# Attention: the local part's steps spread over three more places on three engines, column sums, scores and transposes one step later on TensorE

## The chip, the cores and the metric

The kernel runs on one core of a Trainium2 chip. The metric is the device time of one execution, in microseconds (us). The kernel before took 2866.6 us (median of 3 runs, 2866.42 to 2877.24).

The engines are TensorE (PE in the profile; PEld is its weight load), VectorE (DVE), ScalarE (ACT), GpSimd (POOL) and SyncE (SP), which only issues the weight DMAs here. Each works through its own list of instructions in program order and waits on semaphores that the others raise.

## The reference, cut to what matters

The program is two transformer-like blocks of two layers each, on 512 tokens of width 1024. The change touches the attention of the second block alone. Each of its two layers has 8 heads of stick-breaking attention and 8 heads of local ("sliding window") attention with a sink:

```python
def stick_breaking_attention(q, k, v):      # 8 heads of 64
    z = q @ k.T * scale                      # per block of 128 queries
    log_keep = where(strict, -softplus(z), 0)
    tail = cumsum(log_keep, reverse=True) - log_keep
    w = where(strict, exp(log_sigmoid(z) + tail), 0)
    return w @ v

def sliding_window_sink_attention(q, k, v, sinks):   # window 128
    scores = where(valid, q @ k_band.T * scale, -inf)
    probs = softmax(concat([scores, sink]))[..., :-1]
    return probs @ v_band

for l in range(DEPTH):
    h = rms_norm_2(x, mix_norm_g[l])
    sb_q, sb_k, sb_v, sw_q, sw_k, sw_v, gate_logits = split(h @ w_in[l])
    y_sb = stick_breaking_attention(sb_q, sb_k, sb_v) @ w_branch_sb[l]
    q = apply_rope(rms_norm_2(sw_q, q_norm_g[l])); k = apply_rope(rms_norm_2(sw_k, k_norm_g[l]))
    y_swa = sliding_window_sink_attention(q, k, sw_v, sinks[l]) @ w_branch_swa[l]
    x = x + (gate0 * y_sb + gate1 * y_swa) @ w_out[l]
    x = x + square(relu(rms_norm_2(x, mlp_norm_g[l]) @ w_up[l])) @ w_down[l]
```

## The kernel before, in words

All activations stay on chip, transposed: 128 channels on the partitions, 512 tokens along the row. Weights come in units of 128x1024 elements. SyncE loads a unit, ScalarE rounds it to its high part (`w_hi`, line 882), VectorE subtracts to get the low part (`w_lo`, line 1350), and TensorE makes each product in three matmuls: high by high, low by high, high by low (lines 399 to 401). A unit is 24 such matmuls.

An attention layer works through four pairs, numbered 0 to 3, each with two heads of the stick-breaking part (`stick`) and two of the local part (`window`, its heads called half 0 and half 1). Beside them run the projections that later work needs, the fill: five units in each pair, cut into 20 parts of 6 matmuls. When a unit is done, ScalarE makes a `w_hi` and VectorE stores the result (line 1826) and makes a `w_lo`.

The three are Python generators, and every `yield` ends a step. `interleave` gives step i of n the place `first + (last - first) * (i + 1) / n` on a line from 0 to 1, sorts all steps by place, and writes the instructions out in that order. It is called on TensorE, ScalarE and VectorE separately, with the same numbers. `STICK_STEPS` is 21 over 0 to 1, `WINDOW_STEPS` is 17 over 0 to 0.8, and the fill has 20 over 0.1 to 1. So the order on each engine is fixed by how many steps come before an instruction in its generator.

The steps of `window`, with their lines on the page:

- ScalarE squares the local queries (L1250) once VectorE has stored the pair's fourth unit; TensorE sums over the columns (L775); ScalarE makes the inverse root (L890, L892).
- VectorE scales the queries (L1779) and rotates them in six operations (L1767 to L1773); TensorE makes the scores (L789 to L794).
- VectorE takes the maximum (L1790, L1793); ScalarE the exponentials (L1263, L1265); VectorE the probabilities (L1798 to L1803); TensorE transposes them (L805); ScalarE copies them (L1271); TensorE makes the output (L811, L812); ScalarE copies it (L1275). Then half 1 does the same from the scores on.

The steps of `stick` are the transposes of v (L726), and for each of 8 tiles, n = 0 to 7, of 128, 256, 384 and 512 columns twice over: logits (L736, L737) after the copies of q and k (L1738, L1739), three ScalarE operations (L1229 to L1233, in the text e(n)), the softplus on VectorE (L1747), sums (L1755), the log weights (L745, L748), their exponential (L1238), and the output (L756).

Of the kernel before, what the change touches and what calls it, by code (L numbers as in the profile page):

```python
# [136 lines left out]
class Done:  # L137
# [5 lines left out]
    def mark(self, *event):  # L143
        self.n += 1
        self.plan[event] = self.n
        return self.sem, 1
# [4 lines left out]
    def now(self):  # L151
        return self.sem, self.n
# [28 lines left out]
class Kernel:  # L181
# [47 lines left out]
    def vcol(self, name, i=0, n=1):  # L229
        at = VEC[name] + i  # L230
        return self.vec[:, at:at + n]
# [112 lines left out]


STICK_STEPS = 1 + 2 * (2 * TC + 1) + 1 + 1
WINDOW_STEPS = 2 + 2 + 2 * 6 + 1
STICK_ORDER = [(half, j) for half in range(2) for j in reversed(range(TC))]
Z_BANK_OF = {2: 0, 4: 2, 5: 1, 6: 4, 7: 3}

# [1 line left out]
def filling(fill, parts):  # L352
    for _ in range(parts - 1):
        fill.part()
        yield
    fill.part()


def pair_tasks(stick, window, fill):
    return ((stick, STICK_STEPS, 0, 1), (window, WINDOW_STEPS, 0, 0.8),  # L360
            (filling(fill, len(fill.units) * PARTS), len(fill.units) * PARTS, 0.1, 1))


# [14 lines left out]
def score_view(k, n):  # L378
    return k.bank[6 + n // 2][:, (n % 2) * 2 * P:(n % 2) * 2 * P + 2 * P]
# [10 lines left out]
def pe_program(k):  # L390
# [380 lines left out]

    def window(layer, m):
        at = (layer, m)
        pe.wait_ge(*act_done.at("wq_sq", *at))
        pe.matmul(bank[6][:], k.halves, k.sq, start=True, stop=True).then_inc(*mark("wq_sum", *at))  # L775
        yield
        yield
        yield
        yield
        for half in range(2):  # L780
            r = slice(half * 64, half * 64 + 64)
            if half == 0:
                pe.wait_ge(*dve_done.at("wq", *at))
            else:
                pe.wait_ge(*act_done.at("wo", *at, 0))
            for n in range(TC):
                s = score_view(k, n)
                if n == 0:
                    pe.matmul(s[:, 0:P], k.id_b[:], k.mask_b[:, P:2 * P], start=True, stop=True)  # L789
                    pe.matmul(s[:, P:2 * P], k.id_b[:], k.mask_b[:, 3 * P:4 * P], start=True, stop=False)  # L790
                    mm = pe.matmul(s[:, P:2 * P], k.wq[r, 0:P], k.wk[r, 0:P], start=False, stop=True)
                else:
                    pe.matmul(s, k.id_b[:], k.mask_b[:, 2 * P:4 * P], start=True, stop=False)
                    mm = pe.matmul(s, k.wq[r, n * P:n * P + P], k.wk[r, (n - 1) * P:(n + 1) * P],  # L794
                                   start=False, stop=True)
            mm.then_inc(*mark("scores", *at, half))
            yield
            yield
            yield
            yield  # L800
            pe.wait_ge(*dve_done.at("probs", *at, half))
            for n in range(TC):
                for s in range(2):
                    to = ((n % 2) * 2 + s) * P
                    mm = pe.transpose(bank[6 + n // 2][:, to:to + P], k.p_t[:, n, s * P:s * P + P], k.ident)  # L805
            mm.then_inc(*mark("pT", *at, half))
            yield
            pe.wait_ge(*act_done.at("pT", *at, half))
            for n in range(TC):
                if n > 0:  # L810
                    pe.matmul(bank[6][r, n * P:n * P + P], k.wvt[:, n - 1, r], k.pT[:, n, 0:P], start=True, stop=False)  # L811
                mm = pe.matmul(bank[6][r, n * P:n * P + P], k.wvt[:, n, r], k.pT[:, n, P:2 * P], start=n == 0,  # L812
                               stop=True)
            mm.then_inc(*mark("wo", *at, half))
            yield
# [53 lines left out]
def act_program(k):  # L869
# [18 lines left out]
    def inverse_root(dst, src, scale, *event):  # L888

        act.activation(dst, src, ACT.Ln, scale=scale, bias=k.eps_col[:]).then_inc(*mark())  # L890
        act.wait_ge(*now())
        act.activation(dst, dst, ACT.Exp, scale=-0.5).then_inc(*mark(*event))  # L892
# [354 lines left out]
    def window(layer, m):  # L1247
        at = (layer, m)
        act.wait_ge(*dve_done.at("fill", UNIT["pair", layer, m, 3]))
        act.activation(k.sq, k.lands[3][:], ACT.Square).then_inc(*mark("wq_sq", *at))  # L1250
        yield
        act.wait_ge(*pe_done.at("wq_sum", *at))
        inverse_root(k.rstd[:], bank[6][:], 1.0 / 64, "wq_root", *at)
        yield
        yield
        yield
        for half in range(2):
            r = slice(half * 64, half * 64 + 64)
            yield
            yield  # L1260
            act.wait_ge(*dve_done.at("max", *at, half))
            for n in range(TC):
                act.activation(k.p_t[:, n, :], score_view(k, n), ACT.Exp, bias=k.st[:, 1, n:n + 1],  # L1263
                               accum_out=k.st[:, 2, n:n + 1]).then_inc(*mark())
            act.activation(k.st[:, 3, :], k.st[:, 1, :], ACT.Exp,  # L1265
                           bias=vcol("sinks2", layer * 8 + m + half * 4)).then_inc(*mark("exps", *at, half))
            yield
            yield
            act.wait_ge(*pe_done.at("pT", *at, half))
            for b in range(2):  # L1270
                act.activation(k.pT[:, 2 * b:2 * b + 2, :], bank[6 + b][:].rearrange("p (n s) -> p n s", n=2),  # L1271
                               ACT.Copy).then_inc(*mark("pT", *at, half))
            yield
            act.wait_ge(*pe_done.at("wo", *at, half))
            act.activation(k.wo[r, :], bank[6][r, :], ACT.Copy).then_inc(*mark("wo", *at, half))  # L1275
            yield
        act.wait_ge(*now())
        act.activation(k.y_hi[:, m + 4, :], k.wo[:], ACT.Copy).then_inc(*mark("att_y", layer, m + 4))
# [60 lines left out]
def dve_program(k):  # L1339
# [128 lines left out]
    def rope(x, rot, hd):  # L1468
        dve.wait_ge(*now())
        dve.tensor_tensor(rot[0:64, :], x[64:128, :], k.sin128[64:128, :], ALU.mult).then_inc(*mark())  # L1470
        dve.wait_ge(*now())
        dve.tensor_tensor(rot[64:128, :], x[0:64, :], k.sin128[0:64, :], ALU.mult).then_inc(*mark())
        dve.wait_ge(*now())
        dve.tensor_tensor(x[:], x[:], k.cos128[:], ALU.mult).then_inc(*mark())
        dve.wait_ge(*now())
        dve.tensor_tensor(x[:], x[:], rot[:], ALU.add).then_inc(*mark("rope", hd))
# [298 lines left out]
    def window(layer, m):  # L1775
        at = (layer, m)
        yield
        dve.wait_ge(*act_done.at("wq_root", *at))
        dve.scalar_tensor_tensor(k.wq[:], k.lands[3][:], vcol("q_gain2", layer), k.rstd[:], ALU.mult,  # L1779
                                 ALU.mult).then_inc(*mark())  # L1780
        yield
        rope(k.wq, k.rot).then_inc(*mark("wq", *at))
        yield
        yield
        for half in range(2):
            yield
            sink = vcol("sinks2", layer * 8 + m + half * 4)
            dve.wait_ge(*pe_done.at("scores", *at, half))
            for b in range(2):
                dve.tensor_reduce(k.st[:, 0, 2 * b:2 * b + 2], bank[6 + b][:].rearrange("p (n s) -> p n s", n=2),  # L1790
                                  AX.X, ALU.max).then_inc(*mark())
            dve.wait_ge(*now())
            dve.tensor_scalar(k.st[:, 1, :], k.st[:, 0, :], sink, -1.0, ALU.max,  # L1793
                              ALU.mult).then_inc(*mark("max", *at, half))
            yield
            yield
            dve.wait_ge(*act_done.at("exps", *at, half))
            dve.tensor_tensor(k.st[:, 4, :], k.st[:, 2, :], k.st[:, 3, :], ALU.add).then_inc(*mark())  # L1798
            dve.wait_ge(*now())
            dve.reciprocal(k.st[:, 4, :], k.st[:, 4, :]).then_inc(*mark())  # L1800
            dve.wait_ge(*now())
            for n in range(TC):
                dve.tensor_scalar(k.p_t[:, n, :], k.p_t[:, n, :], k.st[:, 4, n:n + 1], None,  # L1803
                                  ALU.mult).then_inc(*mark("probs", *at, half))
            yield
            yield
            yield
        dve.wait_ge(*act_done.at("att_y", layer, m + 4))
        dve.tensor_tensor(k.y_lo[:, m + 4, :], k.wo[:], k.y_hi[:, m + 4, :].bitcast(F32),
                          ALU.subtract).then_inc(*mark("att_y", layer, m + 4))  # L1810
# [293 lines left out]
```

## Time and profile before

| | before |
|---|---|
| median of 3 runs | 2866.6 us |
| lowest, highest | 2866.42, 2877.24 us |
| the profiled execution | 2872.39 us |
| its span in the trace | 2870.8 us |
| TensorE busy | 2780.5 us (97%), 12462 matmuls |
| VectorE busy | 1509.9 us (53%) |
| ScalarE busy | 1166.3 us (41%) |
| GpSimd busy | 113.0 us (4%) |

The span is the time between the first and the last instruction of the trace; the execution's time has another 1.6 us around it. Busy times are sums of instruction durations. "Granted clock" is TensorE's clock as a share of full speed, 2.4 GHz, in a stretch; its other level is half of that, 1.2 GHz. A timeline row gives the start, the duration, and in brackets how long the engine was idle before it and who released it.

### The profile page before, as it was taken

What the parts mean: (1) busy time and instruction counts of PE and PEld (TensorE: products, weight loads), DVE (VectorE), ACT (ScalarE), POOL (GpSimd) and SP (SyncE); (2) the same over time, 40 slices, a digit from 0 to 9 for tenths busy, and PEclk for the clock granted to TensorE, in tenths of its full rate; (3) what the DMA queues carried; (4) which work ended last, traced back from release to release, by engine and by line L of the source; (5) the groups of instructions that cost most, each with busy time, mean ns of one, the idle gap of its engine ahead of it and who ended that gap; (6) DMA issues with size and microseconds to landing.
All of it is one profiled execution on the core that took longest, in us unless ns stands there. A gap on an engine that the chain in (4) does not pass through costs nothing.

```text
span 2870.8 us, 30831 instructions
## 1 busy us (share of the span) xinstructions
PE 2780.5 (97%) x12462; PEld 2196.8 (77%) x12462; DVE 1509.9 (53%) x2077; ACT 1166.3 (41%) x1736; POOL 113.0 (4%) x79
## 2 busy tenths in 40 slices
PE   8999999999999999999999999999999999999999
PEld 6888778888877888886555788888865557888887
DVE  4566667565676746575343454343544334543433
ACT  6444344333474424354444433332444444333322
POOL 2333110000010000000000000000000000000000
PEclk9999999999999999999999999999999999999999
DMA  4111112332322322331111222232311112222322
GB/s 165 52 63 52 52 59 96 103 96 96 103 95 94 103 95 96 103 103 59 37 44 37 81 96 95 96 103 96 96 59 37 45 37 81 96 96 96 102 97 74
DMA packets 66812, 235.65 MB, mean 82 GB/s; under 512 B 7408, under 2 KB 8176, under 8 KB 66672
## 3 DMA queue, kind: packets, MB, share of 16 engines
q1 hardware_dynamic: 62064, 226.00, 24.2%
q10 hardware_dynamic: 4608, 7.70, 0.8%
q8 instruction: 99, 1.62, 0.2%
q14 instruction: 41, 0.34, 0.0%
HBM read 231.57 MB, written 2.10 MB: 81 GB/s over the span
## 4 chain that ended last, share of the span: by engine, by line
PE 87%; DVE 5%; ACT 4%; issue 2%; POOL 1%; ACTq 0%; DVEq 0%
PE bank L399 25%; PE bank L401 25%; PE bank L400 25%; PE bank L745 1%; ACT w_hi_k L882 1%; PE bank L794 1%; PE bank L756 1%; DVE w_lo_k L1350 1%; PE bank L736 1%; PE bank L748 1%; PE bank L805 1%; PE bank L549 1%; PE bank L812 1%; POOL q_mix L1907 1%; POOL v_mix L1907 1%
## 5 line engine op out<-in xcount | busy, mean ns | idle before, releaser
L399 PE MATMUL bank<-x_hi_k,w_hi_k 128*128 128x512 f32 x2152 | 874.2, 406 | 16.4 <-DVE x_lo_k L1357 16.0
L401 PE MATMUL bank<-x_hi_k,w_lo_k 128*128 128x512 f32 x2152 | 844.3, 392 | 0.0
L400 PE MATMUL bank<-x_lo_k,w_hi_k 128*128 128x512 f32 x2152 | 842.4, 391 | 0.0
L882 ACT ACTIVATE w_hi_k<-raw_k 128x1024 fp32r<-128x1024 f32 x431 | 454.2, 1058 | 946.3 <-PE bank L401 946.3
L1350 DVE TENSOR_TENSOR w_lo_k<-raw_k,w_hi_k 128x1024 fp32r<-128x1024 f32 x431 | 531.4, 1233 | 183.7 <-ACT w_hi_k L882 183.6
L399 PEld LDWEIGHTS bank<-x_hi_k,w_hi_k 128*128 128x128 f32 x2152 | 407.7, 189 | 105.2 <-DVE x_lo_k L1357 18.6
L401 PEld LDWEIGHTS bank<-x_hi_k,w_lo_k 128*128 128x128 f32 x2152 | 406.4, 189 | 87.2
L400 PEld LDWEIGHTS bank<-x_lo_k,w_hi_k 128*128 128x128 f32 x2152 | 407.5, 189 | 84.6 <-issue 4.1
L399 PE MATMUL bank<-y_hi_k,w_hi_k 128*128 128x512 f32 x1136 | 446.4, 393 | 10.8 <-DVE w_lo_k L1350 7.7
L400 PE MATMUL bank<-y_lo_k,w_hi_k 128*128 128x512 f32 x1136 | 443.2, 390 | 0.0
L401 PE MATMUL bank<-y_hi_k,w_lo_k 128*128 128x512 f32 x1136 | 443.2, 390 | 0.0
L1378 DVE TENSOR_TENSOR h_k<-h_k,bank 128x512 f32<-128x512 f32 x136 | 93.3, 686 | 324.2 <-PE bank L401 323.8
L399 PEld LDWEIGHTS bank<-y_hi_k,w_hi_k 128*128 128x128 f32 x1136 | 214.0, 188 | 57.4 <-DVE w_lo_k L1350 9.0
L401 PEld LDWEIGHTS bank<-y_hi_k,w_lo_k 128*128 128x128 f32 x1136 | 213.9, 188 | 44.9
L400 PEld LDWEIGHTS bank<-y_lo_k,w_hi_k 128*128 128x128 f32 x1136 | 214.1, 188 | 43.9 <-issue 0.2
L1876 DVE SCALAR_TENSOR_TENSOR rel_att<-bank,scale_k 128x512 f32<-128x512 f32 x64 | 44.3, 692 | 158.9 <-PE bank L401 158.9
L1747 DVE SCALAR_TENSOR_TENSOR sp_t_att<-bank,e_t_att 128x128 f32<-128x128 f32 (+1 forms) x64 | 31.3, 489 | 90.5 <-ACT e_t_att L1233 89.8
L1238 ACT ACTIVATE w_t_att<-bank 128x128 f32<-128x128 f32 (+1 forms) x64 | 28.2, 440 | 118.7 <-PE bank L745 62.5
L1606 DVE SCALAR_TENSOR_TENSOR cv_ffn<-fpad_ffn,vec_k,cv_ffn 128x512 f32<-128x512 f32 x88 | 65.9, 749 | 1.5
L1606 DVE SCALAR_TENSOR_TENSOR cv_att<-fpad_att,vec_k,cv_att 128x512 f32<-128x512 f32 x88 | 65.9, 749 | 1.5
L736 PE MATMUL bank<-q_att,k_att 64*128 64x128 f32 (+3 forms) x128 | 53.5, 499 | 0.0
L1372 DVE TENSOR_TENSOR fpad_att<-bank,scale_k 128x512 f32<-128x512 f32 x44 | 30.3, 688 | 42.3 <-PE bank L401 42.3
(320 smaller groups left out, 2556.6 us busy)
## 6 DMA issues: line engine op xcount, KB each, us to landing
raw_k<-wstream SPq DMA_DIRECT2D x431, 512.0 KB, 3.3
h_k<-xT ACTq DMA_DIRECT2D x8, 256.0 KB, 7.9
outT<-h_k ACTq DMA_DIRECT2D x8, 256.0 KB, 2.8
decay_mix<-constants ACTq DMA_DIRECT2D x4, 256.0 KB, 2.6
levels_mix<-constants ACTq DMA_DIRECT2D x1, 448.0 KB, 9.1
vec_k<-vectors ACTq DMA_DIRECT2D x1, 286.5 KB, 4.5
cos_mix<-constants ACTq DMA_DIRECT2D x1, 256.0 KB, 8.6
sin_mix<-constants ACTq DMA_DIRECT2D x1, 256.0 KB, 8.6
```

Source lines behind the costliest of these rows:

```text
L399: pe.matmul(dst, wh, rh, start=start, stop=False)
L400: pe.matmul(dst, wh, rl, start=False, stop=False)
L401: return pe.matmul(dst, wl, rh, start=False, stop=stop)
L736: pe.matmul(z_view(k, j), k.ak[r, j * P:j * P + P], k.aq[r, j * P:T], start=True, stop=False)
L882: act.activation(k.w_hi[:, u % SPLIT, :], k.raw[:, u % RAW, :], ACT.Copy).then_inc(*hi_done.mark())
L1350: dve.tensor_tensor(k.w_lo[:, u % SPLIT, :], k.raw[:, u % RAW, :], k.w_hi[:, u % SPLIT, :].bitcast(F32), ALU.subtract).then_inc(*k.lo_done ...
L1372: return dve.tensor_tensor(dst, src, k.scale[:], ALU.mult).then_inc(*mark(*event))
L1378: dve.tensor_tensor(k.h[:, m, :], k.h[:, m, :], bank[BANK[name]][:], ALU.add).then_inc(*mark("added", u))
L1606: dve.scalar_tensor_tensor(cv[j][:], pad[j][:, s:s + T], vcol("ffn_conv", w0 + s), cv[j][:], ALU.mult, ALU.add).then_inc(*mark("conv", lay ...
L1747: dve.scalar_tensor_tensor(keys_view(k.sp_t, j), z_view(k, j), 0.0, k.e_t[:, n % 2, 0:T - j * P], ALU.max, ALU.add).then_inc(*mark("softpl ...
L1876: dve.scalar_tensor_tensor(k.rel[:, j, :], bank[i % 4][:], 0.0, k.scale[:], ALU.max, ALU.mult).then_inc(*mark("rel", u))
L1907: pool.tensor_tensor(dst[:], dst[:], k.taps[s], ALU.add).then_inc(*mark("conv", hd, j))
```

## The change

`window` gets three more steps inside and one more at its start, so each of its generators has 21 steps in place of 17, and its last place goes from 0.8 to 0.85. Nothing is added or taken away on any engine; only the order in which the instructions are written out is another. Line numbers below are those of the kernel before; the changed kernel's are 2 to 9 higher in this part.

```diff
@@ -344,7 +344,7 @@
 
 
 STICK_STEPS = 1 + 2 * (2 * TC + 1) + 1 + 1
-WINDOW_STEPS = 2 + 2 + 2 * 6 + 1
+WINDOW_STEPS = 6 + 2 * 7 + 1
 STICK_ORDER = [(half, j) for half in range(2) for j in reversed(range(TC))]
 Z_BANK_OF = {2: 0, 4: 2, 5: 1, 6: 4, 7: 3}
 
@@ -357,7 +357,7 @@
 
 
 def pair_tasks(stick, window, fill):
-    return ((stick, STICK_STEPS, 0, 1), (window, WINDOW_STEPS, 0, 0.8),
+    return ((stick, STICK_STEPS, 0, 1), (window, WINDOW_STEPS, 0, 0.85),
             (filling(fill, len(fill.units) * PARTS), len(fill.units) * PARTS, 0.1, 1))
 
 
@@ -771,8 +771,10 @@
 
     def window(layer, m):
         at = (layer, m)
+        yield
         pe.wait_ge(*act_done.at("wq_sq", *at))
         pe.matmul(bank[6][:], k.halves, k.sq, start=True, stop=True).then_inc(*mark("wq_sum", *at))
+        yield
         yield
         yield
         yield
@@ -794,6 +796,7 @@
                     mm = pe.matmul(s, k.wq[r, n * P:n * P + P], k.wk[r, (n - 1) * P:(n + 1) * P],
                                    start=False, stop=True)
             mm.then_inc(*mark("scores", *at, half))
+            yield
             yield
             yield
             yield
@@ -1254,6 +1257,8 @@
         yield
         yield
         yield
+        yield
+        yield
         for half in range(2):
             r = slice(half * 64, half * 64 + 64)
             yield
@@ -1264,6 +1269,7 @@
                                accum_out=k.st[:, 2, n:n + 1]).then_inc(*mark())
             act.activation(k.st[:, 3, :], k.st[:, 1, :], ACT.Exp,
                            bias=vcol("sinks2", layer * 8 + m + half * 4)).then_inc(*mark("exps", *at, half))
+            yield
             yield
             yield
             act.wait_ge(*pe_done.at("pT", *at, half))
@@ -1775,11 +1781,13 @@
     def window(layer, m):
         at = (layer, m)
         yield
+        yield
         dve.wait_ge(*act_done.at("wq_root", *at))
         dve.scalar_tensor_tensor(k.wq[:], k.lands[3][:], vcol("q_gain2", layer), k.rstd[:], ALU.mult,
                                  ALU.mult).then_inc(*mark())
         yield
         rope(k.wq, k.rot).then_inc(*mark("wq", *at))
+        yield
         yield
         yield
         for half in range(2):
@@ -1802,6 +1810,7 @@
             for n in range(TC):
                 dve.tensor_scalar(k.p_t[:, n, :], k.p_t[:, n, :], k.st[:, 4, n:n + 1], None,
                                   ALU.mult).then_inc(*mark("probs", *at, half))
+            yield
             yield
             yield
             yield
```

First place: TensorE, half 0, around the scores. `wk_att,wq_att` are the scores, `sp_t_att,negs_att` the log weights of tile 0, `q_att,k_att 128x384` the logits of tile 2; `x_hi_k` to `w_lo_k` are the fill. Before:

```order
L401 MATMUL bank<-x_hi_k,w_lo_k 128x512
L789 MATMUL bank<-mask_b_att,id_b_att 128x128
...
L794 MATMUL bank<-wk_att,wq_att 128x256
L745 MATMUL bank<-sp_t_att,negs_att 128x128
L399 MATMUL bank<-x_hi_k,w_hi_k 128x512
...
L401 MATMUL bank<-x_hi_k,w_lo_k 128x512
L736 MATMUL bank<-q_att,k_att 128x384
```

and now:

```order
L401 MATMUL bank<-x_hi_k,w_lo_k 128x512
L745 MATMUL bank<-sp_t_att,negs_att 128x128
L399 MATMUL bank<-x_hi_k,w_hi_k 128x512
...
L401 MATMUL bank<-x_hi_k,w_lo_k 128x512
L791 MATMUL bank<-mask_b_att,id_b_att 128x128
...
L796 MATMUL bank<-wk_att,wq_att 128x256
L736 MATMUL bank<-q_att,k_att 128x384
```

The log weights and one part of the fill stood behind the scores and stand ahead of them now, so the logits follow the scores directly.

Second place: VectorE, half 0, from the maximum to the probabilities. `st_att<-bank` is the maximum, `p_t_att` the probabilities, `sp_t_att<-bank` the softplus of tiles 2 (384) and 3 (512). Before:

```order
L1790 TENSOR_REDUCE st_att<-bank 128x2 x2
L1793 TENSOR_SCALAR st_att<-st_att,vec_k 128x4
L1747 SCALAR_TENSOR_TENSOR sp_t_att<-bank,e_t_att 128x384
L1755 TENSOR_TENSOR sp_t_att<-sp_t_att 128x128
L1798 TENSOR_TENSOR st_att<-st_att 128x4
L1800 RECIPROCAL st_att<-st_att 128x4
L1803 TENSOR_SCALAR p_t_att<-p_t_att,st_att 128x256 x4
L1747 SCALAR_TENSOR_TENSOR sp_t_att<-bank,e_t_att 128x512
```

and now:

```order
L1753 SCALAR_TENSOR_TENSOR sp_t_att<-bank,e_t_att 128x384
L1798 TENSOR_REDUCE st_att<-bank 128x2 x2
L1801 TENSOR_SCALAR st_att<-st_att,vec_k 128x4
L1761 TENSOR_TENSOR sp_t_att<-sp_t_att 128x128
L1753 SCALAR_TENSOR_TENSOR sp_t_att<-bank,e_t_att 128x512
L1806 TENSOR_TENSOR st_att<-st_att 128x4
L1808 RECIPROCAL st_att<-st_att 128x4
L1811 TENSOR_SCALAR p_t_att<-p_t_att,st_att 128x256 x4
```

The maximum went behind the softplus of tile 2, and the probabilities behind that of tile 3.

Third place: ScalarE, half 1, where the exponentials (`p_t_att,st_att`) meet a `w_hi`. Before:

```order
L1263 ACTIVATE p_t_att,st_att<-bank,st_att 128x256 x4
L1265 ACTIVATE st_att<-st_att,vec_k 128x4
L1238 ACTIVATE w_t_att<-bank 128x128
L882 ACTIVATE w_hi_k<-raw_k 128x1024
L1229 ACTIVATE e_t_att<-bank 128x384
```

and now:

```order
L1241 ACTIVATE w_t_att<-bank 128x128
L885 ACTIVATE w_hi_k<-raw_k 128x1024
L1268 ACTIVATE p_t_att,st_att<-bank,st_att 128x256 x4
L1270 ACTIVATE st_att<-st_att,vec_k 128x4
L1232 ACTIVATE e_t_att<-bank 128x384
```

The exponentials of half 1 went behind the `w_hi`, which waits for a unit of the fill.

## Rows read from the trace of the kernel before

**Rows 1.** Waits on TensorE (PE), whole span: total us, times, longest.

```profile
PE bank L789 <- DVE wq_att L1773: 14.6, 8, 1.8
PE bank L805 <- DVE p_t_att L1803: 14.2, 13, 1.5
PE bank L775 <- ACT sq_k L1250: 13.8, 8, 1.7
```

**Rows 2.** Windows: stretch, length, busy us (count) PE, PEld, DVE, ACT, POOL, clock, DMA.

```profile
1318.61:1387.94 69.33, 63.98 (x264) 40.90 (x264) 27.39 (x52) 30.87 (x68) 0.00 (x0) 0.95 0.12 39
1387.94:1459.88 71.94, 66.90 (x265) 42.66 (x265) 27.40 (x52) 30.97 (x68) 0.00 (x0) 0.91 0.11 37
1459.88:1526.45 66.57, 61.01 (x264) 39.29 (x264) 27.39 (x52) 30.76 (x68) 0.00 (x0) 1.00 0.12 40
2110.60:2180.04 69.44, 63.99 (x264) 40.81 (x264) 27.40 (x52) 30.87 (x68) 0.00 (x0) 0.95 0.12 38
2180.04:2246.62 66.58, 61.01 (x264) 39.29 (x265) 27.40 (x52) 30.75 (x68) 0.00 (x0) 1.00 0.12 40
2315.74:2385.00 69.26, 65.42 (x271) 42.31 (x272) 27.03 (x52) 30.44 (x68) 0.00 (x0) 0.95 0.12 39
...
1396.94:1402.24 5.30, 5.30 (x14) 2.36 (x14) 0.27 (x1) 0.00 (x0) 0.00 (x0) 0.53 0.00 0
```

**Rows 3.** Timeline of TensorE, pair 2: start, us, instruction [idle before <- releaser].

```profile
1459.88 1.12 PE L775 MATMUL bank<-sq_k,con_k 128*128 128x512 f32 x2 [1.73 <-ACT sq_k L1250]
...
1461.37 0.48 PE L736 MATMUL bank<-q_att,k_att 64*128 64x128 f32 x2
...
1468.87 0.23 PE L789 MATMUL bank<-mask_b_att,id_b_att 128*128 128x128 bf16 x1 [1.82 <-DVE wq_att L1773]
...
1472.03 0.49 PE L745 MATMUL bank<-sp_t_att,negs_att 128*128 128x128 f32 x2
...
1473.84 0.91 PE L736 MATMUL bank<-q_att,k_att 64*128 64x384 f32 x2
...
1481.58 1.09 PE L805 MATMUL bank<-con_k,p_t_att 128*128 128x128 f32 x8 [0.53 <-DVE p_t_att L1803]
...
1482.50 0.81 PE L745 MATMUL bank<-sp_t_att,negs_att 128*128 128x384 f32 x2
...
1485.07 0.43 PE L812 MATMUL bank<-pT_att,wvt_att 128*64 128x128 f32 x2
...
1501.26 0.91 PE L736 MATMUL bank<-q_att,k_att 64*128 64x384 f32 x2
...
1505.26 1.09 PE L805 MATMUL bank<-con_k,p_t_att 128*128 128x128 f32 x8 [1.49 <-DVE p_t_att L1803]
...
1508.33 0.43 PE L812 MATMUL bank<-pT_att,wvt_att 128*64 128x128 f32 x2
...
1510.00 1.12 PE L736 MATMUL bank<-q_att,k_att 64*128 64x512 f32 x2
```

**Rows 4.** Timeline of ScalarE (ACT), the same pair.

```profile
1476.03 0.53 ACT L1233 ACTIVATE e_t_att<-e_t_att 128x384 f32<-128x384 f32 x1
...
1477.82 0.47 ACT L1263 ACTIVATE p_t_att<-bank,st_att 128x256 f32<-128x256 f32 x1 [1.26 <-DVE st_att L1793]
...
1480.08 0.61 ACT L1229 ACTIVATE e_t_att<-bank 128x512 f32<-128x512 f32 x1
...
1501.43 1.06 ACT L882 ACTIVATE w_hi_k<-raw_k 128x1024 fp32r<-128x1024 f32 x1 [1.18 <-PE bank L401]
```

**Rows 5.** Timeline of VectorE (DVE), the same pair.

```profile
1460.81 0.42 DVE L1739 COPY k_att<-land_k_att 128x512 f32<-128x512 f32 x1
...
1476.24 1.28 DVE L1790 TENSOR_REDUCE st_att<-bank 128x2 f32<-128x512 f32 x2
...
1479.96 0.16 DVE L1798 TENSOR_TENSOR st_att<-st_att 128x4 f32<-128x4 f32 x1 [1.32 <-ACT st_att L1265]
...
1482.05 0.69 DVE L1747 SCALAR_TENSOR_TENSOR sp_t_att<-bank,e_t_att 128x512 f32<-128x512 f32 x1 [0.53 <-ACT e_t_att L1233]
```


## The prediction

> **What bounds the kernel now.** I read the page's busy table first: TensorE is busy nearly all the span, every other engine about half of it or less, so only what TensorE waits for, or how fast it is clocked, can move the time. Then the waits of TensorE. In the attention there are three, and the change moves the instruction behind each: the column sum waits for the squares (13.8 us, 8 times 1.73), the scores for the rotated queries (14.6 us, 8 times 1.82), the transposes for the probabilities (14.2 us, 13 times) [rows 1]. They make 42.6 us, which no reordering can exceed by waits alone.
>
> Then the windows, one for each pair from its column sum to the next one's. They show a second loss. Two pairs ran at a granted clock of 1.00 all through and took 66.57 and 66.58 us, so a pair without disturbance is the same to a hundredth. The others show 0.95 or 0.91: 69.33, 69.44 and 71.94 us [rows 2]. The last pair of each layer has no next column sum and shows 0.95 too; the remaining one, pair 2 of layer 1, reads as pair 0 does. So TensorE fell to 1.2 GHz in six of eight pairs. Where it falls is in the first scores: those of pair 1 took 5.30 us at 0.53 [rows 2], while those of pair 2, from 1468.87 to 1472.03, took 3.16 us [rows 3]. What came before each fall was the wait of 1.82 us and then score matmuls that use 64 of the 128 rows.
>
> **The change part by part.** No instruction is added, so all is order. I follow pair 2, which ran at the full clock, and ask at each wait two things: how much TensorE work now stands ahead of it, and how much later the chain on the other engines delivers.
>
> *Column sum.* The transposes of v go ahead of it, into the wait for the squares. But the logits of tile 0 come right after, and they need VectorE's copy of k, which ends at 1460.81 + 0.42 = 1461.23 [rows 5]. They started at 1461.37 [rows 3]. So of the half microsecond hidden, 0.14 us at most is kept and the rest becomes a wait for the copy. I take 0.1 (0 to 0.14).
>
> *Scores, half 0.* The log weights of tile 0 and one part of the fill now come ahead: in the trace they run from 1472.03 to 1473.84, which is 1.81 us [rows 3]. TensorE's array was idle from 1468.87 - 1.82 = 1467.05, so with 1.81 us of work moved in it arrives at 1468.86, when the queries are ready (1468.87). On ScalarE the inverse root no longer stands behind the copy of v, while on VectorE the softplus of tile 0 now precedes the scaling; the two about cancel, and may deliver the queries some 0.1 us sooner. The wait goes, and the logits of tile 2 start 1.8 us sooner (1.8 to 2.0). What is late next is the maximum.
>
> *Transposes, half 0.* From the logits of tile 2 (1473.84) to the transposes it was 7.74 us [rows 3]. Now the chain has more links. e(2) ends at 1476.03 + 0.53 = 1476.56 [rows 4], 2.72 us after the logits. The softplus of tile 2 then goes first (0.69 us for 512 columns [rows 5], so some 0.6 for 384), and the maximum starts 3.3 us after the logits in place of 2.40 (1476.24 [rows 5]). From the maximum to e(3) it is 3.84 us (to 1480.08 [rows 4]), from there to the end of the softplus of tile 3 it is 1482.05 + 0.69 - 1480.08 = 2.66, and only then come the probabilities, 1.62 us up to the transposes (1479.96 to 1481.58 [rows 3, 5]). The sum is 11.4, or 11.2 because a weight exponential no longer stands before e(3). That is 3.5 us later than before. TensorE has more work to do meanwhile: log weights and a part, 1482.50 to 1485.07 = 2.57, and the logits of tile 4 (0.48), about 3.05 [rows 3]. So this wait, 0.53 us before, grows by 0.4 on ends added to starts. Instructions overlap a little at their ends, so 0.1 to 0.7; I take 0.3.
>
> *Scores, half 1.* They waited for nothing and still do not: the copy of the output they need has a fill part of about 1.5 us to hide behind. If that cover failed it would cost 0.6 us a pair.
>
> *Transposes, half 1.* From the logits of tile 6 (1501.26) to the transposes it was 4.00 us [rows 3]; the probabilities stood behind a `w_lo`. Now the exponentials stand behind the `w_hi`: it starts 0.17 after the logits and takes 1.06 (1501.43); the exponentials 2.1 (1477.82 to 1480.08 less a short one); e(6), three times 0.53, is 1.6 [rows 4]; the softplus 0.6; the probabilities 1.62. Together 7.15, that is 3.15 us later. The work moved ahead is log weights and a part, from 1505.26 + 0.92 to 1508.33 = 2.15, and the logits of tile 7, 1.12: 3.27 us [rows 3]. The wait of 1.49 us stays nearly as it is: shorter by 0.1, or by up to 0.4 with overlaps, or longer by 0.1. I take 0.2.
>
> What else is queued behind: the outputs, copies and `y_lo` of the local part come later, but the merge after pair 3 waits last for the stick part's output, as before. The weights' `w_hi` and `w_lo` keep their places among the fill, so SyncE's DMA queue sees nothing.
>
> Sum by waits: 0.1 + 1.8 - 0.3 + 0.2 = 1.8 us a pair (1.0 to 2.4), times 8 = 14.4 us (8 to 19).
>
> *The clock.* A short fall costs 69.33 - 66.57 = 2.76 or 69.44 - 66.57 = 2.87, the long one 71.94 - 66.57 = 5.37 us [rows 2]. Five short and one long are 5 x 2.8 + 5.4 = 19.4 us. The scores of half 1 are the same matmuls, without a wait ahead, and none of the eight came with a fall. Of the other waits, 1.73 us ahead of column sums and up to 1.5 ahead of transposes, with full-width matmuls behind, none brought a fall. So I take it that wait and narrow matmuls are needed together, and that all six go. Bounds are 0 and 19.4; more falls than before are a rival below.
>
> A rule of the Trainium skill speaks against this. "TensorE: Matmul & The Clock Gate", section "HAM oscillation — how this bites in real kernels", blames idle gaps much longer than any of the attention's. By it these waits would not cool the array, taking them out would give nothing back, and the time would be that of the first rival. The same page, "A second HAM failure mode: psum-queue depth-cycling", tells of a kernel whose clock fell by short idles between groups of matmuls. This trace, with six falls right behind waits of 1.82 us, sides with the second.
>
> Total, against the profiled execution: 2872.4 - 14.4 - 19.4 = 2838.6 us. It lies 5.8 us above the median; since undisturbed pairs repeat so closely, I put the spread of the runs down to how many falls each had. With the falls gone the forecast stands for the median too.
>
> **The rivals.** *The clock falls as before.* For it: scores and logits of tile 2 now stand together, over 4 us of narrow matmuls, and the page's first rule. Against it: the second scores. Only the waits are won: 2872.4 - 14.4 = 2858.0, or 2852.2 from the median. If half the falls go, 2848.
>
> *The wait only moves.* The new links (the probabilities behind e(3), the exponentials behind `w_hi`) are longer than I added, and the transposes wait 0.9 us more than I say in each half. For it: both chains now cross ScalarE and VectorE twice more. Against it: every link is in the rows. That takes the 14.4 us back: 2853.0 if the falls go, 2872.4 (2866.6 from the median) if they stay; both within half a percent.
>
> *Slower: the clock falls at the new waits.* The transposes of each half now wait right behind narrow logits, and at the pair's start two waits stand within 3 us around the column sum. If these bring falls of their own, 2838.6 grows by 2.8 each; slower by over 0.5% begins at 2881, with 16 falls, two in every pair, and gives 2838.6 + 16 x 2.8 = 2883. For it: the same company of wait and narrow matmuls as at the falls seen. Against it: those waits are shorter than 1.82, and full-width matmuls follow.
>
> **How the numbers follow.** Half a percent, 14.3 us, is about what the measurement can tell from no change; the bounds are 2852.3 and 2880.9. Chances: the forecast, with at most one fall left, 0.64 (2832 to 2843); some falls left, 2843 to 2850, 0.13; the clock as before 0.11, of which a third is faster; the wait only moves 0.07; slower 0.05. Faster is 0.64 + 0.13 + 0.04 = 0.81, the same 0.14, slower 0.05. The range for 8 in 10 is 2832 to 2855.
>
> **What would show it.** In the changed profile the wait of the scores is gone or below 0.2 us; the column sum waits about 1.2 us, followed by logits that wait some 0.4 for the copy of k; the transposes of half 0 wait 0.7 to 1.2 and those of half 1 about 1.3 to 1.5; the windows show 64.8 us a pair at a clock of 1.00. I am wrong if pairs at full clock take 66 us or more (a chain mis-added), or if the granted clock in a pair is still 0.95 (the fall does not need the wait).

## The result, and the profile after

The kernel after takes 2837.1 us (median of 4 runs, 2833.5 to 2840.5), the kernel before 2871.3 us in the same comparison (4 runs, 2866.4 to 2877.2). The ratio is 0.988, with a 95% interval of 0.985 to 0.991. The forecast was 2838.6. The profiled execution of after took 2840.45 us against 2872.39: 31.9 us less. The total is right, but two of its terms are not, and the rows below show which. A fall of TensorE's clock, below, is a stretch at 1.2 GHz instead of 2.4.

The page after, its busy row and the waits of TensorE in the whole span (total us, times, longest), which answer to [rows 1]:

```profile
PE 2764.4 (97%) x12462; PEld 2196.1 (77%) x12462; DVE 1506.2 (53%) x2077; ACT 1165.1 (41%) x1736; POOL 112.5 (4%) x79
```

```profile
PE bank L399 <- DVE x_lo_k L1363: 16.3, 5, 12.8
PE bank L808 <- DVE p_t_att L1811: 14.2, 16, 1.1
PE bank L776 <- ACT sq_k L1253: 10.3, 8, 1.3
...
PE bank L736 <- DVE k_att L1745: 2.3, 8, 0.3
```

The scores (now L791) are gone from the list. The transposes (L808) wait as long in total as before, in 16 places instead of 13. The column sum (L776) waits 1.3 us instead of 1.73, and behind it the logits wait 0.3 us for the copy of k. The first row lies outside the attention and is as before (16.0).

The windows, pair by pair as in [rows 2], and one stretch inside the first:

```profile
1318.69:1384.00 65.31, 61.96 (x265) 40.81 (x265) 26.95 (x52) 30.70 (x69) 0.00 (x0) 0.97 0.12 41
1384.00:1447.90 63.90, 60.52 (x264) 39.73 (x264) 26.85 (x52) 30.70 (x69) 0.00 (x0) 1.00 0.12 42
...
1320.38:1323.79 3.41, 3.41 (x11) 2.53 (x11) 1.63 (x4) 1.58 (x5) 0.00 (x0) 0.50 0.39 150
```

Pair 1 of each layer runs at the full clock and takes 63.9 us, where it was 66.57 [rows 2]. The other six still hold one fall each, of 3.4 us at 0.50 (1.2 GHz), and take 65.3 us where they can be measured. So falls are left in six pairs, but shorter and cheaper: 65.31 - 63.90 = 1.4 us each. And they have moved. In before all six began in the first scores, 0.3 to 1.8 us behind the wait. Now they begin behind the column sum of a pair's start, at 1320.38 in the window above.

TensorE in pair 1, which answers to [rows 3]:

```profile
1384.00 1.12 PE L776 MATMUL bank<-sq_k,con_k 128*128 128x512 f32 x2 [1.29 <-ACT sq_k L1253]
...
1385.40 0.49 PE L736 MATMUL bank<-q_att,k_att 64*128 64x128 f32 x2 [0.28 <-DVE k_att L1745]
...
1392.72 0.23 PE L791 MATMUL bank<-mask_b_att,id_b_att 128*128 128x128 bf16 x1
...
1395.79 0.80 PE L736 MATMUL bank<-q_att,k_att 64*128 64x384 f32 x2
...
1406.65 1.09 PE L808 MATMUL bank<-con_k,p_t_att 128*128 128x128 f32 x8 [0.71 <-DVE p_t_att L1811]
...
1423.04 0.91 PE L736 MATMUL bank<-q_att,k_att 64*128 64x384 f32 x2
...
1429.87 0.33 PE L808 MATMUL bank<-con_k,p_t_att 128*128 128x128 f32 x1 [1.07 <-DVE p_t_att L1811]
```

The scores start without a wait that the trace counts. They are still held a little: VectorE ends the queries at 1392.66, TensorE starts the scores 0.06 us later, and that is 0.42 us behind the start of the fill matmul ahead of them, where the next matmul mostly follows after 0.23. Experiment 8 comes back to this. The transposes wait 0.71 us in half 0 and 1.07 us in half 1, where it was 0.53 and 1.49 [rows 3].

The chain that half 0's transposes wait for, on VectorE and then on ScalarE:

```profile
1398.43 0.56 DVE L1753 SCALAR_TENSOR_TENSOR sp_t_att<-bank,e_t_att 128x384 f32<-128x384 f32 x1 [3.04 <-ACT e_t_att L1236]
1398.90 1.28 DVE L1798 TENSOR_REDUCE st_att<-bank 128x2 f32<-128x512 f32 x2
...
1404.44 0.69 DVE L1753 SCALAR_TENSOR_TENSOR sp_t_att<-bank,e_t_att 128x512 f32<-128x512 f32 x1 [3.60 <-ACT e_t_att L1236]
1405.05 0.15 DVE L1806 TENSOR_TENSOR st_att<-st_att 128x4 f32<-128x4 f32 x1
```

```profile
1402.29 0.31 ACT L1270 ACTIVATE st_att<-st_att,vec_k 128x4 f32<-128x4 f32 x1
1402.48 0.61 ACT L1232 ACTIVATE e_t_att<-bank 128x512 f32<-128x512 f32 x1
```

ScalarE is done with the exponentials at 1402.29 + 0.31 = 1402.60. VectorE could make the probabilities then, but stands for 3.60 us at the softplus of tile 3, which waits for three more ScalarE operations. The probabilities start at 1405.05, some 2.4 us later, by the order alone. TensorE has other work for most of that time and waits 0.71 us. Experiment 6 puts the probabilities ahead.

### The profile page after: what moved, and what is told of

The parts are those of the page before. It is cut to its first block, busy times and chain, and to the rows that moved or that the text cites. A ratio compares the mean times of both kernels' runs of the same rounds, so it can differ in the third digit from the quotient of the medians.

```text
span 2838.7 us, 30831 instructions
## 1 busy us (share of the span) xinstructions
PE 2764.4 (97%) x12462; PEld 2196.1 (77%) x12462; DVE 1506.2 (53%) x2077; ACT 1165.1 (41%) x1736; POOL 112.5 (4%) x79
## 4 chain that ended last, share of the span: by engine, by line
PE 86%; ACT 5%; DVE 5%; issue 2%; POOL 1%; ACTq 0%; DVEq 0%
PE bank L399 25%; PE bank L401 25%; PE bank L400 25%; PE bank L756 1%; PE bank L796 1%; ACT p_t_att L1268 1%; ACT w_hi_k L885 1%; PE bank L745 1%; DVE w_lo_k L1356 1%; DVE p_t_att L1811 1%; PE bank L736 1%; PE bank L808 1%; PE bank L549 1%; PE bank L815 1%; DVE xr_lru L1644 1%
## 5 line engine op out<-in xcount | busy, mean ns | idle before, releaser
L1232 ACT ACTIVATE e_t_att<-bank 128x128 f32<-128x128 f32 (+1 forms) x64 | 27.8, 435 | 93.8 <-PE bank L737 93.8
L1241 ACT ACTIVATE w_t_att<-bank 128x128 f32<-128x128 f32 (+1 forms) x64 | 27.7, 433 | 65.3 <-PE bank L748 39.3
```

## Experiments

Ten kernels were run. Each ratio is to runs of before that were taken on the same chip beside the kernel; the medians of before lie between 2871.3 and 2875.6 us, so medians of different experiments compare to a few us only, and pairs at full clock much closer. Undisturbed pairs are the windows at clock 1.00.

**1. The scores' step alone** (edit to before). TensorE makes the scores of half 0 one place later, and nothing else changes:

```diff
@@ window on TensorE @@
         yield
+        yield
         yield
@@ behind the scores @@
+            if half == 1:
+                yield
-            yield
```

> The kernel before with one part of the change: on TensorE alone, the scores of half 0 go one step later, behind the log weights of tile 0 and a part of the fill; their transposes stay where they were. ScalarE and VectorE keep their old order. By the links of the trace the scores' wait falls from 1.82 to about 0.1 us, and the transposes of half 0 are no longer waited for (0.5 us saved), since the probabilities are not behind the softplus of tile 3 here. An undisturbed pair takes 66.57 - 2.6 = 64.0 us. If the falls need the scores' wait, none is left: 2831 to 2835. If they need only two waits near each other or any wait, some stay: up to 2842. A theory in which all three moves are needed for the gain: 2855.

Measured: 2832.2 us (2830.4 to 2839.0), ratio 0.986 (0.984 to 0.987). Its windows:

```profile
1318.68:1384.07 65.39, 61.98 (x264) 40.36 (x264) 27.48 (x52) 30.88 (x68) 0.00 (x0) 0.97 0.12 41
1384.07:1447.88 63.81, 60.40 (x264) 39.52 (x265) 27.49 (x52) 30.89 (x68) 0.00 (x0) 1.00 0.12 42
```

This one step holds the whole gain: 66.57 - 63.81 = 2.76 us a pair, against 2.67 for the full change. The other edits bring nothing, 0.1 us a pair the other way, and with them come the falls at the pair's start: in the profiles there is one fall in the attention here, in the first pair's scores, and six in after. This kernel isn't free of falls in every run either: its slowest run, 2839.0 us, shows a granted clock of 0.994, as the profiled run of after does.

**2. The scores' wait of before filled** with full-width work (edit to before). Fourteen transposes of the identity go into a bank that is free there:

```diff
+                pe.wait_ge(*act_done.at("wq_root", *at))
+                for n in range(14):
+                    pe.transpose(ch(bank[7], n % TC), k.ident, k.ident)
```

> The kernel before, with 14 more 128x128 transposes of the identity into an unused bank on TensorE, inside the wait of the first scores (the output is unchanged by them). No order is changed, and the scores start when they did. Theory (the falls of the clock come from the array's idle time ahead of narrow matmuls): the six falls in the attention go, every pair takes 66.6 us at a clock of 1.00, and the time is 19.4 us below the profiled kernel before, about 2853. Rival (the narrow score matmuls alone bring the falls, or they come by chance): pairs at 0.95 as before and 2866 to 2877. If the filler outlasts the wait it costs up to 0.3 us a pair, 2 us.

Measured: 2858.6 us (2857.6 to 2859.1), ratio 0.994 (0.993 to 0.996). Its windows and its wait of the scores (L792 in this kernel):

```profile
1318.08:1386.19 68.11, 64.08 (x278) 41.88 (x278) 27.39 (x52) 30.77 (x68) 0.00 (x0) 0.97 0.11 39
...
2105.80:2172.35 66.55, 62.52 (x279) 40.88 (x279) 27.39 (x52) 30.77 (x68) 0.00 (x0) 1.00 0.12 40
```

```profile
PE bank L792 <- DVE wq_att L1776: 2.3, 8, 0.3
```

The pair's length at the full clock is that of before to 0.03 us, so this kernel changes the clock alone. Its profiled execution took 2859.07 us, 13.3 less than before's. The price I put on before's falls, 19.4 us, less four short ones at 1.6 to 1.9, is 12.8, so the price holds. But I expected none to be left, and the first layer shows four, one in each pair, short, 2.7 to 2.9 us into the scores, behind a wait of 0.3 us. Layer 1, with the same instructions, has none. So with the wait of 1.82 us there were more falls, and longer ones; for a short one it isn't needed.

**3. The pair's start as before, the rest changed** (edit to after). The column sum is a step earlier again, and the scaling of the queries too:

```diff
@@ window on TensorE @@
-        yield
         pe.wait_ge(*act_done.at("wq_sq", *at))
...
+        yield
@@ window on VectorE @@
-        yield
         dve.wait_ge(*act_done.at("wq_root", *at))
...
+        yield
```

> The changed kernel with its pair start put back: on TensorE the column sum ahead of the transposes of v, on VectorE the scaling of the queries ahead of the softplus of tile 0. In the changed kernel the clock fell at the pair's start in six pairs for half as long as before (1.4 us each). Theory: that fall comes from the two waits around the column sum (1.29 and 0.28 us) with only it between; with one wait of 1.73 us ahead of the sum and full-width work behind there is none: pairs of 64.1 us (0.2 more than the changed kernel's undisturbed 63.9) at a clock of 1.00, time 2832 to 2835. Rival (the falls are not tied to the start): pairs of 65.5, 2842.

Measured: 2837.6 us (2836.0 to 2839.2), ratio 0.987 (0.985 to 0.989). A pair at full clock, one with a fall, that fall, and where it begins on TensorE:

```profile
1382.87:1447.05 64.18, 60.49 (x265) 39.76 (x265) 26.96 (x52) 30.71 (x68) 0.00 (x0) 1.00 0.12 41
1447.05:1513.50 66.45, 63.46 (x264) 41.72 (x264) 26.96 (x52) 30.71 (x68) 0.00 (x0) 0.95 0.11 40
...
1458.88:1465.71 6.83, 6.83 (x18) 4.70 (x17) 2.28 (x5) 2.23 (x6) 0.00 (x0) 0.50 0.22 77
```

```profile
1456.04 0.23 PE L791 MATMUL bank<-mask_b_att,id_b_att 128*128 128x128 bf16 x1 [0.20 <-DVE wq_att L1779]
...
1458.57 0.95 PE L796 MATMUL bank<-wk_att,wq_att 64*128 64x256 f32 x2
1459.32 1.48 PE L736 MATMUL bank<-q_att,k_att 64*128 64x384 f32 x2
```

The falls at the pair's start are gone, as they should be. Two others appear, which I hadn't expected. They begin 2.8 us into the scores, at their last matmuls, with 0.20 us of idle ahead; the scores are matmuls of 64 rows with short mask matmuls between them. They last 6.8 us and cost 66.45 - 64.18 = 2.3 us each. With experiment 2 this shows that a wait of 0.2 or 0.3 us ahead of narrow matmuls is enough. That narrow matmuls bring a fall by themselves isn't shown: the scores of half 1 are the same matmuls with nothing ahead of them, and in none of the twelve profiles does a fall begin there.

**4. The pair's start of after filled** with full-width work (edit to after):

```diff
-        for c in range(TC):
-            mm = pe.transpose(ch(bank[5], c), ch(k.lands[2], c), k.ident)
+        for _ in range(3):
+            for c in range(TC):
+                mm = pe.transpose(ch(bank[5], c), ch(k.lands[2], c), k.ident)
```

> The changed kernel with the transposes of v made three times over instead of once, so that TensorE is busy for most of the wait for the squares (the result is the same). Nothing else moves. Theory (idle time at the pair's start brings the fall): no falls, pairs of 63.9 us, 8 us less than the changed kernel's profiled execution, about 2832. Rival (idle time does not matter): pairs of 65.3 and 2837 to 2841.

Measured: 2831.7 us (2831.0 to 2832.2), ratio 0.985 (0.984 to 0.987).

```profile
1318.82:1382.75 63.93, 61.44 (x273) 40.62 (x273) 26.87 (x52) 30.71 (x69) 0.00 (x0) 1.00 0.12 42
```

```profile
PE bank L777 <- ACT sq_k L1254: 3.3, 8, 0.4
```

Six pairs read 63.92 or 63.93 us at 1.00, and the last of each layer shows 1.00 too: no fall in the attention. So the six falls of after need the idle time ahead of the column sum, and the transposes' waits of 0.7 and 1.1 us, which stand in this kernel unchanged, brought none. The four runs lie within 1.2 us, where those of after lie within 7.0. The spread of after's runs goes with the clock: 0.994 in its slowest run and 0.997 in its fastest, which is what a different number of falls would give.

**5. The same place filled with narrow work** (edit to after):

```diff
+        for n in range(6):
+            pe.matmul(ch(bank[5], n % TC), ch(k.lands[2], n % TC)[0:64, :], k.ident[0:64, :], start=True, stop=True)
         for c in range(TC):
```

> The kernel after, with six fp32 matmuls that use 64 of the 128 rows put ahead of the transposes of v, into a bank that is overwritten before anything reads it; they fill the waits at a pair's start (1.29 and 0.28 us) with narrow work. The same place filled with full-width work left no fall and 2831.7 us. If only idle time counts for the clock, this one has no fall at a pair's start either, all pairs take about 63.9 to 64.2 us, and the time is about 2831.7 to 2834 us. If narrow matmuls count as little work too, some of the six falls stay at the pair's start, each 1.4 us or more, and the time is 2834 to 2841 us.

Measured: 2834.7 us (2833.8 to 2835.7), ratio 0.987 (0.985 to 0.988).

```profile
1318.99:1383.69 64.70, 63.33 (x279) 41.78 (x277) 26.87 (x52) 30.89 (x68) 0.00 (x0) 0.97 0.13 41
1383.69:1447.76 64.07, 61.98 (x279) 41.05 (x278) 26.87 (x52) 30.87 (x68) 0.00 (x0) 1.00 0.13 42
```

The median lies 0.7 us inside the band of "narrow counts as little work", yet the windows decide against it: no fall at a pair's start. The time over experiment 4 is 0.15 us a pair, since the filling outlasts the wait, and one short fall in the first pair's scores, which costs 64.70 - 64.07 = 0.6 us. Narrow work in the idle time ended the falls at the pair's start as full-width work did. Whether it keeps the clock less well isn't shown: a fall in the first pair's scores also comes in experiment 6 with full-width filling.

**6. The probabilities a step earlier** on VectorE (edit to after), ahead of the softplus of tiles 3 and 6:

```diff
@@ window on VectorE, behind the maximum @@
-            yield
...
@@ behind the probabilities @@
+            yield
```

> The changed kernel with the probabilities one step earlier on VectorE, in both halves: before the softplus of tile 3 in half 0 and of tile 6 in half 1. Theory (the links of the prediction are right: these softplus steps, which wait for ScalarE's e(3) and e(6), hold up the transposes): both waits of the transposes (0.7 and 1.07 us) go, an undisturbed pair takes 63.9 - 1.8 = 62.1 us, and the time falls by 14 us to about 2823. The clock's falls at the pair's start stay, as the start is untouched. Rival (the exponentials on ScalarE are what is late): the waits shrink by less than half, 2830 or more.

Measured: 2814.8 us (2814.0 to 2815.8), ratio 0.980 (0.978 to 0.982).

```profile
1317.66:1379.39 61.73, 60.13 (x264) 39.58 (x264) 27.09 (x52) 30.48 (x69) 0.00 (x0) 1.00 0.13 43
```

```profile
PE bank L776 <- ACT sq_k L1253: 10.3, 8, 1.3
...
PE bank L736 <- DVE k_att L1745: 2.3, 8, 0.3
```

The transposes wait no more, and the pair is 63.90 - 61.73 = 2.17 us shorter. That is more than the two waits of 0.71 and 1.07 us: TensorE's idle time falls by 1.78 us and its busy time by 0.39. Only one fall is left in the attention, at the start of the last pair, where I had expected the falls to stay and about 2823 us. The start is unchanged, so the same 1.29 us of idle goes with six falls in one kernel and with one in another. The idle time doesn't decide alone, and what else does is open.

With the pair's start filled as in experiment 4 it was the same:

> The kernel of e5_probs_early with the transposes of v made three times over, as in e4_warm_after. If idle time at the pair's start makes the falls and the two effects add: pairs of 62.1 us at a clock of 1.00, about 2817. If the shorter pairs bring falls of another kind (ahead of or in the scores, as two of e3_old_start), 2820 to 2826.

Measured: 2814.5 us (2813.5 to 2816.7), ratio 0.980 (0.977 to 0.982), with pairs of 61.72 us and one short fall in the scores of the first. There was little left to win by filling. That fall has the least idle time ahead of all:

```profile
1320.55:1331.19 10.64, 10.62 (x46) 7.15 (x47) 7.22 (x11) 4.41 (x10) 0.00 (x0) 1.00 0.14 49
1331.19:1334.60 3.41, 3.41 (x9) 2.04 (x8) 0.57 (x2) 1.54 (x3) 0.00 (x0) 0.50 0.50 154
```

In the 10.64 us ahead of it TensorE counts 0.02 us of idle, just before the scores, which start 0.42 us behind the fill matmul ahead of them as in after.

The edit of experiment 1 with the probabilities a step earlier in half 1 alone:

> The kernel of e2_scores_only (the kernel before with the scores of half 0 one step later) with the probabilities of half 1 one step earlier on VectorE, ahead of the store of the fill and its low part. The exponentials end at 1499.1 in the trace of the kernel before and the transposes could start at 1503.6, so their wait of 1.49 us goes: pairs of 63.8 - 1.6 = 62.2 us, 13 us below e2_scores_only, about 2819. Two steps moved from the kernel before then do better than the whole change. Rival (VectorE's store, now later, holds up the fill): part of it is lost, 2823 or more.

Measured: 2820.8 us (2817.8 to 2823.1), ratio 0.982 (0.980 to 0.984): pairs of 62.11 us at full clock, and two long falls in the scores. Neither this kernel nor experiment 6's has a wait ahead of its transposes, and they differ by 62.11 - 61.73 = 0.4 us a pair: that much the change's other steps are worth, once the probabilities stand right.

**7. A failure: the column sum later, the copies of q and k earlier** (edit to experiment 6's kernel). The copies for pairs 1 to 3 go to the end of the pair before, and TensorE's column sum one more place back, behind fill:

```diff
@@ window on TensorE @@
+        yield
         pe.wait_ge(*act_done.at("wq_sq", *at))
...
-        yield
@@ stick on VectorE, last step @@
+        if pair < 3:
+            copies(layer, pair + 1)
```

> The kernel of e5_probs_early with real work in the wait at the pair's start in place of repeats: VectorE copies q and k for pairs 1 to 3 at the end of the pair before, and TensorE's column sum goes behind the logits of tile 0. The wait for the copy of k goes and the logits hide in the wait for the squares: idle time at the start falls from 1.57 to about 0.8 us in six pairs (4.4 us in all); pair 0 of each layer, whose copies stay where they were, loses up to 1.8 us. Without falls 2815 to 2819; if the logits, which use half of the rows, count as idle for the clock, falls stay and it is 2819 to 2827.

Measured: 2828.6 us (2827.9 to 2830.3), ratio 0.985 (0.983 to 0.987).

```profile
PE bank L791 <- DVE wq_att L1785: 7.1, 7, 1.0
```

```profile
1444.89:1506.62 61.73, 60.00 (x264) 39.73 (x265) 26.99 (x52) 30.48 (x69) 0.00 (x0) 1.00 0.13 43
...
2147.33:2212.19 64.86, 63.13 (x264) 41.47 (x264) 27.09 (x52) 30.59 (x69) 0.00 (x0) 0.95 0.13 41
```

The later column sum passes its lateness down the chain to the scores, which wait 1.0 us again, ahead of narrow matmuls. The pair is no shorter, and falls come back: five in the attention, 3.1 us for a long one. In the first pair of each layer, where the copies stay at their old place, the logits now wait 2.7 us for the copy of k.

**8. The same copies, the column sum left alone** (edit to experiment 6's kernel), and the scaling of the queries ahead of the softplus of tile 0:

```diff
@@ window on VectorE @@
-        yield
         dve.wait_ge(*act_done.at("wq_root", *at))
...
+        yield
@@ stick on VectorE, last step @@
+        if pair < 3:
+            copies(layer, pair + 1)
```

> The version with the probabilities ahead of the softplus (2814.8 us), with two waits more taken on: the copies of q and k for pairs 1 to 3 are written at the end of the pair before, and the queries' scaling stands ahead of the softplus of tile 0 on VectorE. Theory (the chain of links): the logits' wait of 0.3 us for the copy of k goes, the scores still wait for nothing, since the scaling keeps its place right behind the root; 61.73 - 0.35 = 61.4 us a pair and 2812 to 2813 us in all. Rival (a lead only moves the next wait): with the copy gone the column sum or the scores wait as much longer, pairs stay at 61.7 us and the time at 2814 to 2816 us; if the scores wait again for 0.5 us or more, falls of the clock come back at 1.6 to 3.2 us each and it is 2818 us or more.

Measured: 2811.0 us (5 runs, 2810.1 to 2812.3), ratio 0.979 (0.977 to 0.980), the fastest of all.

```profile
1381.44:1442.64 61.20, 59.91 (x264) 39.58 (x264) 27.27 (x52) 30.48 (x69) 0.00 (x0) 1.00 0.14 44
...
2080.02:2141.58 61.56, 59.98 (x265) 39.59 (x265) 27.96 (x54) 30.49 (x69) 0.00 (x0) 1.00 0.13 43
```

The window of the second row is a layer's first pair, where the copies are at their old place: there the scaling alone gives 61.73 - 61.56 = 0.17 us, although the trace counted no wait of the scores. It is the hidden one of after: the scores now start 0.23 us behind the matmul ahead of them (2088.34 to 2088.57) instead of 0.42. The copies give another 0.36. I had expected 0.35 together. One fall is left, at the start of the very first pair, one of the two where the logits still wait for the copy of k.

## Why the prediction was right, and where it was wrong

*What bounds the kernel.* Right: only TensorE's waits in the attention and its clock moved. The other engines' busy times are within 4 us of before, and off the path.

*Column sum.* Right in its mechanism: a wait of 1.29 us (1.2 said), then 0.28 us for the copy of k (0.4 said). From the last fill matmul ahead of both to the logits it takes 3.52 us instead of 3.61, a term of +0.09 where I took 0.1.

*Scores, half 0.* The wait went in full. From the first logits to those of tile 2 it was 12.47 us [rows 3]; now the same stretch takes 2.08 us less, where I took 1.8 and gave 2.0 as the end.

*Transposes, half 0.* I put them 11.2 us behind the logits of tile 2. They came 1406.65 - 1395.79 = 10.86 us behind, 3.12 more than the 7.74 of before, with 3.05 us of work moved in. The term is -0.07 instead of -0.3; the wait itself grew by 0.18. The links were right in number and order. I added ends to starts, while two instructions in a row on one engine overlap by 0.1 us or so, which I had named but not taken off in full: the maximum starts 0.09 us ahead of the end of the softplus before it (1398.90 against 1398.99), the probabilities 0.08 ahead of that of tile 3 (1405.05 against 1405.13). And e(2) ended 2.60 us behind the logits instead of 2.72. From one engine to another nothing overlaps: the later instruction starts 0.03 to 0.06 us behind the end of the earlier one.

*Transposes, half 1.* 6.83 us behind the logits of tile 6 instead of 7.15, for the same reason: the exponentials, for one, start 0.10 us ahead of the end of the `w_hi`. The term is +0.4 instead of +0.2, and the wait is 1.07 us, below my 1.3 to 1.5.

*The sum by waits.* The step that failed is "1.8 us a pair (1.0 to 2.4)". It measured 66.57 - 63.90 = 2.67, outside the range, so 21.4 us for eight pairs in place of 14.4. Of the 0.87 that I missed, 0.28 lie in the scores, 0.23 and 0.24 in the transposes of half 0 and half 1, and the rest in stretches to which I gave no term. Both windows give the split by another cut: TensorE's idle time falls from 66.57 - 61.01 = 5.56 us to 63.90 - 60.52 = 3.38, by 2.18, and its busy time by 0.49. I gave busy time no term. The matmuls in the list are the same, and no run isolates why they take less; the rows show two places. A fill matmul ahead of a wait counts its full 0.40 us, and one that is followed closely only the 0.23 to the next start. And the 14 matmuls of the scores up to the next instruction take 3.07 us now, with the logits behind them, and took 3.16 with the log weights behind them [rows 3].

*The clock.* This is the step that was wrong in its mechanism: "I take it that wait and narrow matmuls are needed together, and that all six go". The falls at the scores did go. Six came at the pair's start, where the change put two idle times within 3 us around the column sum. That is the place and the mechanism of my rival "slower", at half its price: 1.4 us each, not 2.8. Of 19.4 us, 19.4 - 6 x 1.4 = 11.0 came back. Experiments 2 and 3 show falls with no wait over 0.3 us ahead; experiment 4 shows that after's six need the idle time at the start, and experiment 6 that it doesn't bring them by itself.

So the sum comes out as 21.4 + 11.0 = 32.4 us against 31.9 measured. The forecast is right to 1.5 us of the median by luck: 7.0 us too little in one term and 8.4 too much in the other cancel. My own sign for this, a granted clock below 1.00 in a pair, is there in six pairs.

The two sections of the Trainium skill that I weighed, "HAM oscillation — how this bites in real kernels" and "A second HAM failure mode: psum-queue depth-cycling" of "TensorE: Matmul & The Clock Gate", part in the same way as before. Experiment 4 bears out the second: taking 0.9 us of idle out of each pair's start ended the falls there. The fall of experiment 6's second kernel, with 0.02 us of idle in the 10.64 us ahead of it, fits neither text as I read it.

## What to carry to other kernels

When the order of several engines' lists moves, follow each chain link by link. Start a link some 0.1 us before the last one's end where both are on one engine, and 0.03 to 0.06 us behind it where they are on two. Count TensorE's busy time as well as its waits: with 2.18 us of idle time went 0.49 us of busy time here, and an instruction can be held for 0.2 us where the trace counts no wait. The one step that crosses the wait is often the whole gain; test it alone, and look at what each further step puts itself behind, since the probabilities behind a softplus cost 22 us here, 17 of them in the length of the pairs, the rest probably in falls. Where TensorE is the bound, price each short idle time with the clock as well, and if it can't be closed, try to fill it with work whose result nobody reads.

## What was not expected of the hardware

- The clock falls at small cause: behind 1.29 us of idle (after), 2.8 us into the scores with 0.20 us of idle ahead (experiment 3), and behind 10.64 us with 0.02 us of idle in them (experiment 6's second kernel). With the same instructions in both layers one had four falls and the other none (experiment 2).
- A fall of 3.4 us mostly costs 1.4 to 1.9 us, once 0.6 (experiment 5); one of 6.8 us costs 2.3 to 3.2.
- Full-width work that nobody reads, 0.9 us of it at each pair's start, took 5 us off the kernel and its spread of runs from 7.0 to 1.2 us (experiment 4).
- Open is why equal pairs differ: why pair 1 of each layer of after has no fall, and why an unchanged pair's start has six falls after and one in experiment 6. The falls aren't tied to the instructions alone: the four of experiment 2 start at 1329.80, 1398.07, 1466.34 and 1534.60, 68.27 us apart each time to a hundredth, while the pairs are 68.11, 68.40 and 68.12 us long. So equal pairs may differ by the moment at which they run; no run here tests that.
